# Groups that end a phase are read earlier, in banks and token halves, in a kernel of two transformer blocks

## The chip, the core and the metric

One core of one Trainium2 chip runs the whole program. Its engines are TensorE (PE), VectorE (DVE), ScalarE (ACT), GpSimd (POOL) and SyncE (SP, which only issues transfers). The metric is the device time of one execution in microseconds (us).

## What is computed

Two different transformer blocks follow each other on 256 tokens of width 2048, all in float32. Cut to what matters here:

```python
def first_block(x, p, ...):
    u = rms_norm(h, ln_mix_pre)
    hq, hf, hi, hg, aq, ak, av = split(u @ w_in)                    # 7 x 1024 columns
    mixed = concatenate([hgrn2(hq, hf, hi, hg), dilated_attention(aq, ak, av)]) @ w_out
    h = h + rms_norm(mixed, ln_mix_post)
    y = conv_gated_mlp(rms_norm(h, ln_ffn_pre), w_up, ..., w_down)  # hidden 5632
    h = h + rms_norm(y, ln_ffn_post)
    return h + (p @ w_pe) * sigmoid(h @ w_pg)

def second_block(x, p, ...):
    z = rms_norm(h, attn_norm_g) @ w_in                             # 5 x 1024 columns
    h = h + concatenate([diff_attention(...), gmlp_gate(...)]) @ w_out
    f = rms_norm(h, ffn_norm_g)
    h = h + (silu(f @ w1) * (f @ w3)) @ w2                          # hidden 5632
    h = h + (p @ pl_w_up) * sigmoid(h @ pl_w_gate)
    return rms_norm(h, final_norm_g)
```

The recurrence of `hgrn2` is computed over the whole sequence by levels: a level compares token spans half as long as the one before, its products are laid into one matrix of scores by `merge`.

## The kernel before

**Phases and chunks.** The weights pass once, in chunks of 1 MB (128 x 2048 values). `PHASES` lists them: `in1`, `out1`, `up`, `down1`, `pe1`, `down1b`, `pg1` for the first block; `in2`, `out2`, `glu`, `down2`, `pe2`, `down2b`, `pg2` for the second. A phase runs `iters` times over `body` chunks; `per` chunks, 4 or 11, make a group, whose sums stay in PSUM (the tensor `ps`, 8 banks of 512 values a partition) until it is complete.

**Each weight is split in two.** Factor and weight are each written as a high part, rounded to fp32r, plus a low part, the rest, and three of the products are summed. SP loads a chunk into one of four `raw` buffers; ACT rounds it into `w_hi` (`high`, L513); DVE subtracts into `w_lo` (`low`, L1370); PE multiplies. `w_hi` and `w_lo` have two buffers each, so the rounding of chunk c + 2 starts when chunk c is multiplied (semaphore `chunks_multiplied`), and must be through `low` before chunk c + 1 ends.

**Two layouts.** Column phases (`up`, `in2`, `glu`, the first four rounds of `in1`) put output columns on partitions: 32 matmuls a chunk, a group takes 4 banks (`by_columns`, L950 and L951). Row phases (the rest) put tokens on partitions: 24 matmuls a chunk, a group takes 2 banks, `2 * gr` for tokens 0 to 127 and the next for 128 to 255 (`by_rows`, L966 to L968, which does both halves for each row tile of weights).

**What reads a finished group.** `mixed_square` (ACT) and `mixed_gains` (DVE) in `out1`, `down1`, `down1b`; after the last of these, `token_sums`, `token_roots`, `inverse_roots`, `mixed_add`, then PE turns the new rows (`turn`, L926) and ACT and DVE split them (`turned_high`, `turned_low`) before the next phase can start. `add_rows` (DVE, L1965) in `out2`, `down2`, `down2b`. `sigmoid` (ACT, L805) and `gate` (DVE, L1839 and L1841) in `pg1`, `pg2`. Before PE writes a group, `group_free` waits until its banks are read.

**Order.** There is no scheduler: every engine runs its own hand-written list. `stream` on each engine walks the chunks j of a phase; on ACT it issues `high` for chunk j + 2 and then what the table `at` has for j; on DVE `low` for j + 2, then `at[j]`, then, where a group ends, the reading of it (`evac`); on PE `at[j]` stands before the matmuls of chunk j. `positions` does the same for `in1` with chunk numbers 0 to 55; `slot(l)` is 18 + 3(l - 1). `level(l)` on PE needs `factors(l)` and `merge(l - 1)`; `attention_scores(n)` needs banks 6 and 7 that `masked(n)` on DVE reads.

## Time and profile before

| | |
|---|---|
| median of 3 runs (lowest to highest) | 2556.55 us (2554.41 to 2558.72) |
| the profiled execution | 2555.99 us, span 2554.3 us |
| mean granted TensorE clock | 0.991 |
| PE busy | 2491.4 us, 98% of the span |
| DVE busy, ACT busy | 1489.6 us, 1096.5 us |
| share of the chain that ended last | PE 93%, DVE 3%, ACT 2% |

The span runs from the first to the last instruction of one profiled execution. "Busy" is the time in which an engine executes something; an engine with a lower share has idle time that costs nothing unless another engine waits for it. The granted clock is in shares of full speed.

### The profile page before, as it was taken

To read this page: it belongs to the slowest core of one execution; us is meant where nothing else is said; L and a number is where in the kernel's file an instruction comes from. 1 tells how busy PE (TensorE), PEld (TensorE's weight loads), DVE (VectorE), ACT (ScalarE), POOL (GpSimd) and SP (SyncE) were. 2 spreads that over 40 slices of the span, in tenths; PEclk is the share of its full clock that TensorE was granted. 3 is DMA by queue.
4 is the path that set the end of the run, shared out by engine and by line. 5 is a ranking of instruction groups with operands and counts; after the bars stand their busy time and mean duration, and the time that the engine had idled before them with its cause. 6 is when DMAs were issued, how large, how long until landed. Compare 5 with 4: busy or idle time off the path is not lost.

```text
span 2554.3 us, 31924 instructions
## 1 busy us (share of the span) xinstructions
PE 2491.4 (98%) x13381; PEld 2144.0 (84%) x13381; DVE 1489.6 (58%) x1069; ACT 1096.5 (43%) x916; POOL 188.7 (7%) x115
## 2 busy tenths in 40 slices
PE   7999999999999999999999999999999999999997
PEld 6998788788888888888788888778888888888886
DVE  5865635566677775444565757545555555545455
ACT  4533455544444444333454435344333333333344
POOL 2000000011212112000000000001121211100000
PEclk9999999999999999999999999999999999999999
DMA  6544455455555555655465554455556555555544
GB/s 230 190 142 140 142 172 181 159 187 184 194 185 193 186 192 186 213 183 196 148 222 162 185 170 144 148 165 183 196 183 194 184 194 186 197 181 198 184 179 148
DMA packets 230532, 460.04 MB, mean 180 GB/s; under 512 B 7526, under 2 KB 10540, under 8 KB 230060
## 3 DMA queue, kind: packets, MB, share of 16 engines
q1 hardware_dynamic: 230152, 458.71, 53.5%
q8 instruction: 69, 1.13, 0.2%
q14 instruction: 19, 0.16, 0.0%
q10 hardware_dynamic: 292, 0.04, 0.0%
HBM read 456.62 MB, written 2.10 MB: 180 GB/s over the span
## 4 chain that ended last, share of the span: by engine, by line
PE 93%; DVE 3%; ACT 2%; issue 1%; DMA 1%; POOL 0%; ACTq 0%; SPq 0%; POOLq 0%; DVEq 0%
PE ps L950 33%; PE ps L951 17%; PE ps L966 12%; PE ps L967 12%; PE ps L968 12%; ACT w_hi L513 1%; PE ps L957 1%; PE ps L959 1%; PE ps L958 1%; DVE w_lo L1370 1%; PE ps L1126 1%; PE ps L926 1%; PE ps L1133 0%; DMA raw<-in_w_down_dram 0%; DMA raw<-in_w_in_dram 0%
## 5 line engine op out<-in xcount | busy, mean ns | idle before, releaser
L1370 DVE TENSOR_TENSOR w_lo<-raw,w_hi 128x2048 fp32r<-128x2048 f32 x428 | 980.3, 2291 | 1010.0 <-ACT w_hi L513 1009.9
L513 ACT ACTIVATE w_hi<-raw 128x2048 fp32r<-128x2048 f32 x428 | 820.4, 1917 | 1372.9 <-PE ps L951 722.4
L950 PE MATMUL ps<-xa,w_hi 128*128 128x512 f32 x3072 | 1071.8, 395 | 12.4 <-DVE xa L1434 6.7
L951 PE MATMUL ps<-xa,w_lo 128*128 128x256 f32 x3072 | 853.7, 278 | 0.0
L950 PEld LDWEIGHTS ps<-xa,w_hi 128*128 128x128 f32 x3072 | 578.3, 188 | 147.6 <-DVE h L1965 5.9
L951 PEld LDWEIGHTS ps<-xa,w_lo 128*128 128x128 f32 x3072 | 579.5, 189 | 0.0
L966 PE MATMUL ps<-w_hi,g 128*128 128x512 f32 x1088 | 427.0, 393 | 2.1 <-DVE w_lo L1370 1.1
L968 PE MATMUL ps<-w_hi,g 128*128 128x512 f32 x1088 | 424.7, 390 | 0.0
L967 PE MATMUL ps<-w_lo,g 128*128 128x512 f32 x1088 | 424.7, 390 | 0.0
L966 PEld LDWEIGHTS ps<-w_hi,g 128*128 128x128 f32 x1088 | 205.2, 189 | 46.1 <-issue 3.0
L968 PEld LDWEIGHTS ps<-w_hi,g 128*128 128x128 f32 x1088 | 205.1, 189 | 43.0
L967 PEld LDWEIGHTS ps<-w_lo,g 128*128 128x128 f32 x1088 | 205.2, 189 | 42.0 <-issue 0.2
L950 PE MATMUL ps<-g,w_hi 128*128 128x512 f32 x640 | 227.8, 400 | 3.1 <-ACT ff L805 3.0
L478 POOL TENSOR_TENSOR ff<-ff 128x1024 f32<-128x1024 f32 x22 | 96.6, 4391 | 1526.6 <-DVE ff L1787 869.5
L951 PE MATMUL ps<-g,w_lo 128*128 128x256 f32 x640 | 179.6, 281 | 0.0
L950 PEld LDWEIGHTS ps<-g,w_hi 128*128 128x128 f32 x640 | 121.4, 190 | 32.5 <-ACT ff L805 3.4
L966 PE MATMUL ps<-w_hi,xa 128*128 128x512 f32 x320 | 126.4, 395 | 0.0
L967 PE MATMUL ps<-w_lo,xa 128*128 128x512 f32 x320 | 125.0, 391 | 0.0
L968 PE MATMUL ps<-w_hi,xa 128*128 128x512 f32 x320 | 125.0, 390 | 0.0
L951 PEld LDWEIGHTS ps<-g,w_lo 128*128 128x128 f32 x640 | 121.9, 190 | 0.3 <-issue 0.2
L1484 DVE TENSOR_REDUCE ff<-ps 128x1024 f32<-128x2048 f32 x44 | 100.5, 2284 | 0.0
L481 POOL TENSOR_TENSOR g<-ff,g 128x1024 f32 x22 | 74.4, 3382 | 107.0 <-ACT g L759 107.0
(275 smaller groups left out, 1599.5 us busy)
## 6 DMA issues: line engine op xcount, KB each, us to landing
raw<-in_ffn_w_dram SPq DMA_DIRECT2D x132, 1024.0 KB, 5.1
raw<-in_w_in_dram SPq DMA_DIRECT2D x96, 1024.0 KB, 5.1
raw<-in_w_up_dram SPq DMA_DIRECT2D x88, 1024.0 KB, 5.0
raw<-in_w_down_dram SPq DMA_DIRECT2D x44, 1024.0 KB, 5.0
raw<-in_w_out_dram SPq DMA_DIRECT2D x32, 1024.0 KB, 5.0
raw<-in_w_pg_dram SPq DMA_DIRECT2D x16, 1024.0 KB, 5.1
raw<-in_pl_w_gate_dram SPq DMA_DIRECT2D x16, 1024.0 KB, 5.9
raw<-in_w_pe_dram SPq DMA_DIRECT2D x2, 1024.0 KB, 4.8
```

The costliest lines, as they stand in the source:

```text
L478: pool.tensor_tensor(prod[:, :, :], ff_out[0][:, :, :], val[:, :, :], ALU.mult)\
L481: pool.tensor_tensor(g[:, bass.ds(i * 4, 4), S:2 * S], prod[:, :, :], g[:, bass.ds(i * 4, 4), 0:S].bitcast(F32), ALU.subtract).then_inc(se ...
L513: A(w_hi[j % SPLIT][:, :], raw[s][:, :], ACT.Copy).then_inc(sem("w_hi_ready"), 1)
L926: last = nc.tensor.transpose(bank(turn_bank(q), 2)[:, k * S + a * P:k * S + (a + 1) * P], h_rows[:, a, (4 * q + k) * P:(4 * q + k + 1) * P ...
L950: mm(ps[:, 4 * gr + n, :], hi[:, k, w], x, start=begin, stop=False)
L951: return mm(ps[:, 4 * gr + n, 0:S], lo[:, k, w], x[:, 0:S], start=False, stop=end)
L957: mm(o, hi[:, k, w], x[:, 0:S], start=begin and n % 2 == 0, stop=False, skip_group_check=True)
L966: mm(o, high, hi, start=begin, stop=False)
L967: mm(o, high, lo, start=False, stop=False)
L968: last = mm(o, low, hi, start=False, stop=end)
L1370: V.tensor_tensor(w_lo[j % SPLIT][:, :], raw[j % RAW][:, :], w_hi[j % SPLIT][:, :].bitcast(F32), ALU.subtract).then_inc(sem("w_lo_ready"), 1)
L1484: return V.tensor_reduce(dst, halves(gr).rearrange("p b (a t) -> p b t a", a=2), AX.X, ALU.add)
```

## The change

It moves instructions and waits; what is computed stays.

1. In the last chunk of every group of a row phase PE does all matmuls of the first token half, raises `half_multiplied`, then those of the second half. ACT's first square of a mixed group waits for that; both squares of a group now come before the gains of their bank, and after the last group of `out1` and `down1b` the second gain product stands behind the first `mixed_add`.
2. A column phase's first group waits at its start only for the older pair of the row phase's banks (`rows_done(ph, 3)`), and for the younger ones (`rows_done(ph, 4)`) before its third quarter, where it first writes them.
3. `stream(..., early=True)` on DVE (`out2`, `down2`, `down2b`): `add_rows` stands ahead of `low` where a group ends. In `pg1`, ACT's last sigmoid stands ahead of the last rounding.
4. In `in1` the attention scores move from positions 33, 36, 39 to 34, 37, 40, behind the level there; `masked` and the last `merge` move with them.
5. The last group of `pg2` is read in halves, and two of the four stores of the output are issued by ACT instead of SP.

```diff
-            def mixed_square(name, n, gr, chunks):
+            def mixed_square(name, n, gr, chunks, half):
 
                 m = 4 * (name == "down1") + n
                 o = square_out[name]
                 if n:
                     act.wait_ge(sem("mixed_squared"), 2 * m)
+                act.wait_ge(sem("half_multiplied"), half)
+                A(o[:, 0:512], bank(2 * gr), ACT.Square, accum_out=sum_at(name, 0, n)).then_inc(sem("mixed_squared"), 1)
                 act.wait_ge(sem("chunks_multiplied"), chunks)
-                A(o[:, 0:512], bank(2 * gr), ACT.Square, accum_out=sum_at(name, 0, n)).then_inc(sem("mixed_squared"), 1)
-                act.wait_ge(sem("mixed_gained"), m + 1)
...
-                41: lambda: exponentials(2, p0),
+                42: lambda: exponentials(2, p0),
...
-            stream("pg1", unroll=True, started=True, at={
+            stream("pg1", unroll=True, started=True, late=True, at={
                 0: steps({1: lambda: row_squares("in2", 1)}),
                 1: steps({1: lambda: turned_high("in2", 1)}),
                 3: lambda i: sigmoid("pg1", 2 * i),
                 4: lambda i: row_squares("in2", 2 * i),
                 5: lambda i: turned_high("in2", 2 * i),
-                7: lambda i: sigmoid("pg1", 2 * i + 1)})
+                7: steps({0: lambda: sigmoid("pg1", 1)})})
+            sigmoid("pg1", 3)
+            high("pg1", 1, 9)
...
-                7: lambda i: sigmoid("pg2", 2 * i + 1)})
+                7: steps({0: lambda: sigmoid("pg2", 1)})})
+            act.wait_ge(sem("h_ready"), H_READY["out"] + 2)
+            for a in range(2):
+                act.wait_ge(*((sem("chunks_multiplied"), done("pg2", 1, 7)) if a else (sem("half_multiplied"), HALVES["pg2"] + 4)))
+                A(sigmoids["pg2"][1][:, 512 * a:512 * (a + 1)], bank(2 + a), ACT.Sigmoid).then_inc(sem("last_sigmoid"), 1)
             root_table()
-            row_squares("out", 3)
+            act.wait_ge(sem("rows_squared"), ROWS_SQUARED["out"] + 3)
+            for a in range(2):
+                act.wait_ge(sem("last_added"), a + 1)
+                A(square_out["out"][:, 512 * a:512 * (a + 1)], row_quad(h_rows, 3)[:, a, :], ACT.Square, accum_out=sum_at("out", a, 3))\
+                    .then_inc(sem("last_squared"), 1)
...
+                act.wait_ge(sem("out_rows"), half + 1)
+                act.dma_start(out[0, P:S, half * 1024:(half + 1) * 1024], o).then_inc(sem("out_stored"), 16)
...
-                    pe.wait_ge(*{"up": (sem("factor_ready"), FACTOR["up"] + 1), "in2": (sem("sigmoid_done"), 4),
-                                 "glu": (sem("h_ready"), H_READY["glu"] + 4)}[ph])
+                    rows_done(ph, 3)
...
+                            if begun and ph in COLUMN_PHASES and (j, n) == (0, 2):
+                                rows_done(ph, 4)
                             if begun and ph in COLUMN_PHASES and (j, n) == (4, 3):
                                 pe.wait_ge(sem("scale_ready"), SPREAD[ph])
+                            if rows and q < per - 1:
+                                for a in range(2):
+                                    last = by_rows(2 * gr, x[:, x0 + n, :], hi[:, n, :], lo[:, n, :], q == 0 and n == 0, False, a)
+                                continue
+                            if rows and n % 2 == 0:
+                                for k in range(4):
+                                    last = by_rows(2 * gr, x[:, x0 + k, :], hi[:, k, :], lo[:, k, :], False, k == 3, n // 2)
+                                if n == 0:
+                                    last.then_inc(sem("half_multiplied"), 1)
...
-                33: lambda: attention_scores(0),
-                slot(5) + 4: lambda: level(5),
-                36: lambda: attention_scores(1),
-                slot(6) + 4: lambda: level(6),
-                39: lambda: attention_scores(2),
-                slot(7) + 4: lambda: level(7),
+                slot(5) + 4: lambda: (level(5), attention_scores(0)),
+                slot(6) + 4: lambda: (level(6), attention_scores(1)),
+                slot(7) + 4: lambda: (level(7), attention_scores(2)),
...
+            def mixed_gain(name, n, gr, a):
 
                 m = 4 * (name == "down1") + n
                 c = slice(512 * n, 512 * (n + 1))
+                dve.wait_ge(sem("mixed_squared"), 2 * m + a + 1)
+                last = V.tensor_tensor(y_rows[name][:, a, c], bank(2 * gr + a), gain_row[name][:, c], ALU.mult)
+                if a:
+                    last.then_inc(sem("mixed_read"), 1)
+
+            def mixed_gains(name, n, gr):
+
                 dve.wait_ge(sem("gain_row_landed"), 16 * GAIN_ROW_NO[name])
-                V.tensor_tensor(y_rows[name][:, 1, c], bank(2 * gr + 1), gain_row[name][:, c], ALU.mult).then_inc(sem("mixed_gained"), 1)
-                dve.wait_ge(sem("mixed_squared"), 2 * m + 1)
-                V.tensor_tensor(y_rows[name][:, 0, c], bank(2 * gr), gain_row[name][:, c], ALU.mult).then_inc(sem("mixed_read"), 1)
-                if n == 3:
-                    dve.wait_ge(sem("mixed_squared"), 2 * m + 2)
-                    token_sums(name)
+                mixed_gain(name, n, gr, 0)
+                if n < 3:
+                    return mixed_gain(name, n, gr, 1)
+                dve.wait_ge(sem("mixed_squared"), 8 * (name == "down1") + 8)
+                token_sums(name)
...
+                        if early and j % per == per - 1:
+                            dve.wait_ge(sem("chunks_multiplied"), chunk_no(ph, i, j) + 1)
+                            evac(i, j // per)
...
-                34: lambda: (factors(6), masked(1, p1[:, 0:4, :], S)),
-                35: lambda: merge(5),
+                34: lambda: factors(6),
+                35: lambda: (masked(1, p1[:, 0:4, :], S), merge(5)),
                 slot(7): lambda: relative(7),
-                37: lambda: (factors(7), masked(2, p1[:, 4:8, :], S)),
-                38: lambda: merge(6),
+                37: lambda: factors(7),
+                38: lambda: (masked(2, p1[:, 4:8, :], S), merge(6)),
                 39: lambda: maxima(2, p1, 8),
-                40: lambda: (masked(3, p0, P), maxima(3, p0, 0)),
-                41: lambda: merge(7),
+                41: lambda: (masked(3, p0, P), maxima(3, p0, 0), merge(7)),
...
+            mixed_gain("out1", 3, 1, 1)
...
+            stream("out2", lambda i, gr: add_rows("out2", 2 * i + gr, gr), unroll=True, started=True, early=True,
...
+            stream("pg2", lambda i, gr: gate("pg2", 2 * i + gr) if (i, gr) != (1, 1) else None,
...
-            final_gain(3).then_inc(sem("final_gained"), 1)
-            row_sums("out")
+            for a in range(2):
+                dve.wait_ge(sem("last_sigmoid"), a + 1)
+                g3 = sigmoids["pg2"][1][:, 512 * a:512 * (a + 1)]
+                then(V.tensor_tensor(g3, g3, pe_rows["pe2"][3][:, 512 * a:512 * (a + 1)], ALU.mult))
+                hq = row_quad(h_rows, 3)[:, a, :]
+                V.tensor_tensor(hq, hq, g3, ALU.add).then_inc(sem("last_added"), 1)
+            for a in range(2):
+                dve.wait_ge(sem("last_added"), a + 1)
+                last = V.tensor_tensor(row_quad(final_rows, 3)[:, a, :], row_quad(h_rows, 3)[:, a, :],
+                                       gain_row["out"][:, 1536:2048], ALU.mult)
+            last.then_inc(sem("final_gained"), 1)
+            dve.wait_ge(sem("rows_squared"), ROWS_SQUARED["out"] + 3)
+            dve.wait_ge(sem("last_squared"), 2)
+            token_sums("out")
```

**in1.** PE at positions 33 and 34 before; L1133 are the scores, L1126 a level, L966 to L968 a chunk.

```order
L968 MATMUL ps<-w_hi,xa 128x512
L1133 MATMUL ps<-g_work 128x256 [waits level_merged,banks_read]
L1133 MATMUL ps<-g_work 128x256 x3
L966 MATMUL ps<-w_hi,xa 128x512 [waits w_lo_ready,factor_ready]
...
L1126 MATMUL ps<-g_work 128x64 [waits level_merged,level_factors]
L1126 MATMUL ps<-g_work 128x64 x15
```

The same place of the changed kernel, and its position 37; L1153 is a level there, L1160 the scores, L976 to L978 a chunk.

```order
L978 MATMUL ps<-w_hi,xa 128x512
L1153 MATMUL ps<-g_work 128x64 [waits level_merged,level_factors]
L1153 MATMUL ps<-g_work 128x64 x15
L1160 MATMUL ps<-g_work 128x256 [waits level_merged,banks_read]
L1160 MATMUL ps<-g_work 128x256 x3
L976 MATMUL ps<-w_hi,xa 128x512 [waits w_lo_ready,factor_ready]
...
L1153 MATMUL ps<-g_work 128x64 [waits level_merged,level_factors]
L1153 MATMUL ps<-g_work 128x64 x15
L1160 MATMUL ps<-g_work 128x256 [waits att_masked]
L1160 MATMUL ps<-g_work 128x256 x3
```

The scores stand behind the level. On DVE, positions 34 and 35 before: L1631 and L1632 are `factors`, L1665 `masked`, L1370 `low`, L1650 `merge`.

```order
L1370 TENSOR_TENSOR w_lo<-raw,w_hi 128x2048 [waits w_hi_ready]
L1631 TENSOR_TENSOR g_work<-g_work,ff 128x512x2 [waits level_decay]
L1632 TENSOR_TENSOR g_work<-g_work 128x512x2
L1665 SCALAR_TENSOR_TENSOR ff<-ps,g_work 128x1024 [waits att_scores]
L1370 TENSOR_TENSOR w_lo<-raw,w_hi 128x2048 [waits w_hi_ready]
L1650 COPY_PREDICATED g_work<-g_work,ps 128x256x4 [waits level_merged,level_done]
```

And of the changed kernel, where these are L1664 and L1665, L1698, L1394 and L1683:

```order
L1394 TENSOR_TENSOR w_lo<-raw,w_hi 128x2048 [waits w_hi_ready]
L1664 TENSOR_TENSOR g_work<-g_work,ff 128x512x2 [waits level_decay]
L1665 TENSOR_TENSOR g_work<-g_work 128x512x2
L1394 TENSOR_TENSOR w_lo<-raw,w_hi 128x2048 [waits w_hi_ready]
L1698 SCALAR_TENSOR_TENSOR ff<-ps,g_work 128x1024 [waits att_scores]
L1683 COPY_PREDICATED g_work<-g_work,ps 128x256x4 [waits level_merged,level_done]
```

`masked` is now behind the next `low`, directly ahead of `merge`.

**out2 to glu.** DVE at the end of `out2` before; L1965 is `add_rows`, L1434 the split of a factor for `glu`.

```order
L1434 SCALAR_TENSOR_TENSOR xa<-ps,cols,xa 128x256 [waits factor_high]
L1434 SCALAR_TENSOR_TENSOR xa<-ps,cols,xa 128x256 x3
L1370 TENSOR_TENSOR w_lo<-raw,w_hi 128x2048 [waits w_hi_ready] x2
L1965 TENSOR_TENSOR h<-h,ps 128x2x512 [waits chunks_multiplied]
L1370 TENSOR_TENSOR w_lo<-raw,w_hi 128x2048 [waits w_hi_ready]
L1434 SCALAR_TENSOR_TENSOR xa<-ps,cols,xa 128x256 [waits factor_high]
L1434 SCALAR_TENSOR_TENSOR xa<-ps,cols,xa 128x256 x3
```

Of the changed kernel, with `add_rows` as L1999 and the split as L1464:

```order
L1464 SCALAR_TENSOR_TENSOR xa<-ps,cols,xa 128x256 [waits factor_high]
L1464 SCALAR_TENSOR_TENSOR xa<-ps,cols,xa 128x256 x3
L1394 TENSOR_TENSOR w_lo<-raw,w_hi 128x2048 [waits w_hi_ready]
L1999 TENSOR_TENSOR h<-h,ps 128x2x512 [waits chunks_multiplied]
L1394 TENSOR_TENSOR w_lo<-raw,w_hi 128x2048 [waits w_hi_ready] x2
L1464 SCALAR_TENSOR_TENSOR xa<-ps,cols,xa 128x256 [waits factor_high]
L1464 SCALAR_TENSOR_TENSOR xa<-ps,cols,xa 128x256 x3
```

`add_rows` stands ahead of one of the two `low` that it was behind.

**pg1 to in2.** ACT at the end of `pg1` before; L805 is the sigmoid, L513 `high`.

```order
L513 ACTIVATE w_hi<-raw 128x2048 [waits chunks_multiplied,raw_landed0]
L513 ACTIVATE w_hi<-raw 128x2048 [waits chunks_multiplied,raw_landed1]
L805 ACTIVATE ff<-ps 128x1024 [waits h_ready,chunks_multiplied]
L513 ACTIVATE w_hi<-raw 128x2048 [waits chunks_multiplied,raw_landed2]
L554 ACTIVATE g<-ps,cols 128x256 [waits turned]
```

Of the changed kernel, with the sigmoid as L804 and `high` as L512:

```order
L512 ACTIVATE w_hi<-raw 128x2048 [waits chunks_multiplied,raw_landed0]
L804 ACTIVATE ff<-ps 128x1024 [waits h_ready,chunks_multiplied]
L512 ACTIVATE w_hi<-raw 128x2048 [waits chunks_multiplied,raw_landed1]
L512 ACTIVATE w_hi<-raw 128x2048 [waits chunks_multiplied,raw_landed2]
L553 ACTIVATE g<-ps,cols 128x256 [waits turned]
```

The last sigmoid is ahead of the last `high` of `pg1`.

## Rows read from the trace of the kernel before

**Rows 1.** The page: busy time and instructions of PE.

```profile
PE 2491.4 (98%) x13381; PEld 2144.0 (84%) x13381; DVE 1489.6 (58%) x1069; ACT 1096.5 (43%) x916; POOL 188.7 (7%) x115
```

**Rows 2.** PE's waits: line, for whom, us in total, times, longest.

```profile
PE ps L926 <- DVE h L1416: 7.5, 2, 3.8
...
PE ps L950 <- DVE h L1965: 5.5, 1, 5.5
PE ps L950 <- ACT ff L805: 3.0, 1, 3.0
PE ps L1133 <- DVE ff L1665: 2.4, 1, 2.4
PE ps L1139 <- DVE ff L1665: 2.4, 1, 2.4
PE ps L1133 <- DVE g_work L1560: 2.3, 1, 2.3
...
PE ps L966 <- DVE ff L1808: 1.2, 1, 1.2
```

**Rows 3.** Windows: us; PE, PEld, DVE, ACT, POOL busy; PE clock; DMA share, GB/s.

```profile
233.80:238.50 4.70, 4.67 (x14) 3.77 (x15) 3.35 (x2) 0.00 (x0) 0.00 (x0) 0.64 0.47 144
1345.20:1351.20 6.00, 5.94 (x19) 5.07 (x20) 4.00 (x5) 0.01 (x1) 0.96 (x3) 0.50 0.61 200
1706.40:1709.60 3.20, 3.18 (x10) 2.69 (x11) 0.00 (x0) 0.00 (x0) 0.00 (x0) 0.50 0.96 310
2548.00:2553.30 5.30, 0.00 (x0) 0.00 (x0) 0.00 (x0) 0.74 (x1) 0.00 (x0) 0.50 0.98 391
```

**Rows 4.** Timeline, out2 to glu: start, us, engine, line, operation, [idle before].

```profile
1701.00 1.91 ACT L513 ACTIVATE w_hi<-raw 128x2048 fp32r<-128x2048 f32 x1 [3.52 <-PE ps L968]
...
1702.95 2.29 DVE L1370 TENSOR_TENSOR w_lo<-raw,w_hi 128x2048 fp32r<-128x2048 f32 x1 [3.14 <-ACT w_hi L513]
1705.15 1.21 DVE L1965 TENSOR_TENSOR h<-h,ps 128x1024 f32<-128x1024 f32 x1
```

**Rows 5.** Timeline, pg1 to in2, and a later chunk of in2.

```profile
1344.20 1.00 ACT L805 ACTIVATE ff<-ps 128x1024 f32<-128x1024 f32 x1
...
1344.33 2.29 DVE L1370 TENSOR_TENSOR w_lo<-raw,w_hi 128x2048 fp32r<-128x2048 f32 x1 [3.14 <-ACT w_hi L513]
...
1347.79 1.23 DVE L1841 TENSOR_TENSOR h<-h,ff 128x1024 f32<-128x1024 f32 x1
...
1377.53 1.92 ACT L513 ACTIVATE w_hi<-raw 128x2048 fp32r<-128x2048 f32 x1 [3.63 <-PE ps L951]
```

**Rows 6.** Timeline of DVE in in1: mask of the scores, and merges.

```profile
235.90 1.25 DVE L1650 COPY_PREDICATED g_work<-g_work,ps 128x1024 f32<-128x1024 uint32 x1
...
258.48 1.22 DVE L1665 SCALAR_TENSOR_TENSOR ff<-ps,g_work 128x1024 f32<-128x1024 f32 x1
...
261.81 1.26 DVE L1650 COPY_PREDICATED g_work<-g_work,ps 128x1024 f32<-128x1024 uint32 x1
...
286.15 2.46 DVE L1650 COPY_PREDICATED g_work<-g_work,ps 128x1024 f32<-128x1024 uint32 x1
```

**Rows 7.** Timeline of ACT and DVE, out1 to up.

```profile
486.66 0.60 ACT L533 ACTIVATE g_work<-ps 128x512 f32<-128x512 f32 x1 [2.01 <-PE ps L968]
...
487.32 0.60 ACT L535 ACTIVATE g_work<-ps 128x512 f32<-128x512 f32 x1
...
488.77 4.06 DVE L1416 SCALAR_TENSOR_TENSOR h<-g_work,tok,h 128x512 f32<-128x512 f32 x6
493.19 1.66 DVE L1434 SCALAR_TENSOR_TENSOR xa<-ps,cols,xa 128x256 fp32r<-128x256 f32 x4 [0.35 <-ACT xa L554]
```

**Rows 8.** Timeline of the end; issues of the stores (ns min/median/max).

```profile
2540.76 1.02 ACT L805 ACTIVATE g_work<-ps 128x1024 f32<-128x1024 f32 x1 [8.90 <-PE ps L968]
...
2545.83 0.16 DVE L1378 TENSOR_REDUCE tok<-tok 128x2 f32<-128x8 f32 x1 [0.20 <-ACT g_work L543]
...
L380 SPq DMA_DIRECT2D out_dram<-g_work x4: 357/608/1191, 2547.3 to 2549.0; - x4
```

More of the change, by code:

```diff
@@ L29 @@
 NORMS = {"out1": 6, "down1": 20, "up": 34, "in2": 48, "glu": 62, "out": 76}
+HALVES = {"out1": 6, "down1": 10, "down1b": 12, "pg1": 14, "out2": 18, "down2": 22, "down2b": 24, "pg2": 26}
 NORM_NO = {"out1": 1, "up": 2, "down1": 3, "in2": 4, "glu": 5, "out": 6}
@@ L376, in _ @@
             for half in range(2):
[L377 to L381 removed]
+                sp.wait_ge(sem("out_rows_too"), half + 1)
+                c = slice(half * 1024, (half + 1) * 1024)
+                sp.dma_start(out[0, 0:P, c], final_rows[:, 0, c]).then_inc(sem("out_stored"), 16)
             sp.wait_ge(sem("out_stored"), 64)
@@ L959, in by_narrow_columns, with by_rows @@
                 return mm(o, lo[:, k, w], x[:, 0:S], start=False, stop=end, skip_group_check=True)
[L961 to L969 removed]
+            def by_rows(b, x, hi, lo, begin, end, a):
+                high, low = x[:, a * P:(a + 1) * P], x[:, S + a * P:S + (a + 1) * P]
+                o = bank(b + a)
+                mm(o, high, hi, start=begin, stop=False)
+                mm(o, high, lo, start=False, stop=False)
+                return mm(o, low, hi, start=False, stop=end)
             def mixed_done(n):
@@ L1447, in first, with stream @@
                 return lambda i: f() if isinstance(i, int) and i == 0 else None
-            def stream(ph, evac=None, peel=0, at=None, unroll=False, tail=0, started=False, before=None):
+            def stream(ph, evac=None, peel=0, at=None, unroll=False, tail=0, started=False, before=None, early=False):
                 pl = plan[ph]
@@ L1476, in body @@
                             at[j](i)
-                        if evac and j % per == per - 1:
+                        if evac and not early and j % per == per - 1:
                             dve.wait_ge(sem("chunks_multiplied"), chunk_no(ph, i, j) + 1)
```

47 lines of the change are left out of this document (19 added, 28 removed).

## The prediction

> **What bounds the kernel now.** I read the page first: PE is busy 2491.4 us of 2554.3 [rows 1], so what a change of order can win is in the 63 us in which PE has nothing, and in stretches at the lower clock. The table of PE's waits names them [rows 2]: 5.5 us at the first chunk of `glu` for `add_rows` (L1965), 3.0 at the first of `in2` for the last sigmoid (L805), 2.4, 2.4 and 2.3 at the attention scores in `in1`, 7.5 in two waits for `mixed_add` (L1416, borders `out1`/`up` and `down1b`/`pg1`), 1.2 in `pe2`. Then the windows behind three of these waits, for what a wait costs once it is over [rows 3]: after the wait in `in2` PE runs 6.0 us at granted clock 0.50, the lower of its two levels (1.2 of 2.4 GHz); after that in `glu` 3.2 us at 0.50; after the first score wait 4.7 us at 0.64. Half of 6.0 is lost, 3.0 us; half of 3.2, 1.6; and 0.36 of 4.7, 1.7. So a wait that goes takes such a stretch with it.
>
> **The grid.** At `out2`'s last chunk ACT starts the next rounding at 1701.00, 1.91 long after 3.52 idle: a row chunk is 5.43 us, and this start marks its end within 0.1 [rows 4]. DVE starts `low` 1.95 later and its next instruction 4.15 after the mark. A column chunk is 1.92 + 3.63 = 5.55 [rows 5].
>
> **out2 to glu** [rows 4]. Before, `low` stands ahead of `add_rows`, which ends at 1706.4. With `early` it stands first: from 1701.0 to 1702.2, while DVE would wait for ACT until 1702.95 anyway, so `low` isn't moved. PE now asks at its start only for the older pair of banks, and for the other after half a chunk, at 1703.7, when it has been free for 1.5 us. The next chunk's `w_lo` comes at 1705.2 and is needed at 1706.4. Wait 5.5 and slow stretch 1.6 go: **7.1 us**. If the order were back, 5.4 less half a chunk (2.8) would still wait.
>
> **pg1 to in2** [rows 5]. The last chunk of `pg1` ended 1.95 before `low` started, at 1342.4. With `late`, the sigmoid of 1.0 stands first on ACT, and ends at 1343.4; PE asks for it only half a chunk on, at 1345.1. Queued behind it are the last rounding of `pg1`, 0.9 later than before, then `low` (to 1347.5), the load that SP starts when `low` frees its raw buffer (wanted three chunks later), and the gate, two instructions of 1.23, which now ends at 1349.9 instead of 1349.0. PE reaches its second chunk at 1342.2 + 5.55 = 1347.75: 0.2 us in hand. `turn("in2", 3)`, a chunk and a half after the start, is at 1350.5 and needs the gate of 1349.9: 0.6 in hand. Wait 3.0 and slow stretch 3.0 go: **6.0 us**. What is late next is this turn; a slip there would cost its own size.
>
> **in1** [rows 4, 6]. All three waits for scores go (2.3 + 2.4 + 2.4 = 7.1), and so does the slow stretch of 1.7. But the merge of a level is now behind `masked` on DVE, and `level` is the next thing PE wants. One chunk's mark is 0. `low` runs from 1.95 to 4.15, `masked` takes 1.2 (L1665) to 5.3, and `merge(5)` with its 1.26 ends at 6.55; PE is at `level(6)` at 5.35, so it waits 1.2. `merge(6)` is 2.46 long, so `level(7)` waits 2.4. `merge(4)`, which before lay under a wait, ends at 237.15, and PE without that wait is there at 236.9 (231.5 + 5.43): 0.2. At position 41 `masked`, `maxima` and `merge(7)` (1.2, as much for `maxima`, which reads as many elements, and 2.4 by the row of `merge(6)`) now follow each other: the next `low` starts at 9.0 and ends at 11.3, and is needed at 10.8: 0.5. New waits are 4.3 us. Net 7.1 + 1.7 - 4.3 = **4.5 us**; 2.8 if the wait of 2.4 drops the clock as the first one did. The scores themselves, 8 to 16 matmuls, are the same in number. Two similar waits of 2.4 dropped nothing, so I take 4.5.
>
> A rule for this, in sentences of their own. The Trainium skill, TensorE: Matmul & The Clock Gate, section "Part 1: The HAM clock gate", says that the number of slow matmuls after a start is run-variable, one kernel showing 6, 11 or 14. The trace agrees: the wait of 3.0 us cost 3.0 in clock, that of 5.5 only 1.6. By the rule the 6.3 us of clock in my sum are one draw, and another execution could lose two more or less.
>
> **out1 to up, down1b to pg1** [rows 7]. The two squares of the last group start 0.66 us apart (486.66, 487.32). With the first bank finished half a chunk earlier, only the second follows the last matmul, so the sums come 0.66 sooner. But one of the two gain products moves behind the first `mixed_add`: 0.68 more among the six adds of 0.68 (4.06 / 6), ahead of `turned_low`. At `up`, `turned_low` stood 0.35 idle for ACT after the adds (L1434) and can start 0.3 earlier: **0.3 us**. At `pg1` ACT's part is one instruction for four, so that DVE, with its longer queue, is the later: **0**. Bounds for each are 0 and 0.66. The waits of up to 3.8 and their slow clock stay.
>
> **down2 to pe2** [rows 2]. `add_rows` leaves the queue ahead of the first copy out of the banks (L1808), which so comes 1.1 us earlier; of the wait of 1.2 some 0.05 stays: **1.1 us**. In `pe1` the products are still behind `low`, and the wait of 1.2 stays. `down2b` has no wait to lose.
>
> **The end** [rows 8]. The last sigmoid is split, but DVE's stream still waits for the whole last chunk before it turns to either half. From 2540.76 it then has four half-width products and sums of 0.70 each (0.68 for the adds of that width in [rows 7], and a wait on the one before), to 2543.5, and two gain products of some 0.65, to 2544.8; `token_sums` stood at 2545.83. ACT's table load and its two squares fit beside (the last square follows the last sum and ends at 2544.3). So **1.0 us**. The stores: two of four now go from ACT. The output leaves at DMA share 0.98 from 2548.0 to 2553.3 [rows 3], so more issuers add nothing, and the first issue is SP's in both; the second ACT product now starts after an issue (0.36 to 1.2 us), yet its data is wanted only 4 us into the stores. Nothing lost or won; bounds -0.5 and +1. The Trainium skill, DMA: Bandwidth & Descriptors, section "Issuing engines are not separate DMA queues", says the same: only the sequencer's time for the issue is saved.
>
> **Last chunks by token halves.** 30 chunks of 24 matmuls stay as many, but a bank now takes 12 in a row instead of 3. Column chunks keep a bank for 8 and need 5.55 for the columns that a row chunk does in 5.43 [rows 4, 5]; laid wholly on this, it is 0.12 x 30 = 3.6 us at most. The other reading, that the 32 instead of 24 instructions make it, is as near: I take 0 and keep 3.6 for the range.
>
> **Sum.** 7.1 + 6.0 + 4.5 + 0.3 + 0 + 1.1 + 1.0 = 20.0 us. The profiled execution has 2555.99 (span 2554.3), 0.56 under the median of the runs shown, 2556.55. Less 20.0: 2536.0, and on the median's footing **2536.5 us**.
>
> **Rivals.**
> - The clock: the new wait of 2.4 in `in1` brings its own slow stretch (1.7), or a border that now runs through still drops. 2538 to 2541. One wait of three such did; chance 0.2.
> - Moved waits: the small margins of 0.2 and 0.6 at `in2` don't hold, or the last chunks cost up to 3.6. For it speaks that DVE is there nearly continuously in use; against it that a slip costs only itself. 2538 to 2540; chance 0.1.
> - The borders are given back: PE starts `glu` and `in2` early but stands later for the scale, which hangs on the same row sums. Then 7.1 + 6.0 return: 2549.6. Against it: the last turn stands at PE's own position in the second chunk and starts that chain, before and after. Chance 0.05.
> - No effect (within 0.2%, 5.1 us, about what a measurement of this kernel can tell): the above and the clock together; 0.03.
> - Slower: long runs in one bank slow the matmuls in the last chunks. To eat 20 us it must cost 0.67 us in each of 30, 28 ns on a step of 227; to be slower by 5.1, 35 ns, and then 2562. The column chunks, with runs of 8, show at most 5 ns. Chance 0.02.
> - Better than forecast: stores on two queues, and clock at the borders of `up` and `pg1`, some 1 to 3 us: 2534. Chance 0.1.
>
> The forecast as worked out, 2535 to 2538, has 0.5. The range 2532.5 to 2541.5 takes in the clock, the moved waits and the better case. Faster 0.95, same 0.03, slower 0.02.
>
> **What would show it.** In the table of waits, the rows of L1965 and L805 are gone, and PE's first `glu` and `in2` windows are at clock 1.0. In `in1` the score rows are gone, and `level` waits for the merge (COPY_PREDICATED) twice, 1.2 and 2.4 us. `mixed_add` still holds 6 to 7 us. The span from the last matmul to the end is 1 us shorter. I am wrong if PE waits at a later chunk of `in2` or `glu`, if row chunks that end a group last over 5.5 us, or if `level` waits show a granted clock under 1.

## The result and the profile after

| | before | after |
|---|---|---|
| median (lowest to highest), 5 runs each | 2558.56 us (2554.41 to 2559.83) | 2544.37 us (2543.28 to 2546.19) |
| the profiled execution | 2555.99 us, span 2554.3 | 2543.82 us, span 2542.1 |
| mean granted TensorE clock | 0.991 | 0.990 |

The ratio is 0.9949, interval [0.9934, 0.9963]: faster, by less than forecast. On the two profiled executions it is 12.2 us instead of 20.0. The page of the kernel after, then its table of PE's waits (line, what it waited for, us in total, times, longest):

```profile
PE 2492.3 (98%) x13381; PEld 2146.2 (84%) x13381; DVE 1490.2 (59%) x1072; ACT 1096.6 (43%) x917; POOL 193.1 (8%) x115
```

```profile
PE ps L961 <- DVE xa L1464: 7.3, 3, 3.5
...
PE ps L937 <- DVE h L1446: 6.9, 3, 3.0
PE ps L1153 <- DVE g_work L1683: 4.2, 3, 2.5
PE ps L1345 <- ACT xa_work L855: 2.1, 1, 2.1
PE ps L1355 <- ACT ff L871: 2.0, 1, 2.0
PE ps L976 <- DVE w_lo L1394: 2.0, 3, 0.9
...
PE ps L976 <- DVE xa_work L1841: 1.2, 1, 1.2
```

Against [rows 2]: `add_rows` and the sigmoid are gone, so is the `ff` of `pe2`, and so are the three scores. New is `level` (L1153) waiting for `merge` (L1683), 4.2 us in three waits where 3.8 were forecast; the waits of row chunks for `w_lo` grew from 1.1 to 2.0, by 0.9 with 0.5 forecast. PE is busy 0.9 us longer than in [rows 1], though its matmuls are as many: some of them ran slower.

**Where the 12.2 us are.** Every chunk has one rounding on ACT, so the starts of the 428 roundings are one scale for both traces. The difference of these starts (after less before), taken between stretches:

| stretch | forecast | measured |
|---|---|---|
| `in1` | -4.5 | +2.7 |
| border of `up` | -0.3 | +0.7 |
| `up` to `down1b`, border of `pg1` | 0 | +0.2 |
| border of `in2` | -6.0 | -5.9 |
| within `in2` and `out2` | 0 | -0.6 |
| border of `glu` | -7.1 | -7.1 |
| `pe2` | -1.1 | -1.1 |
| behind the last rounding | -1.0 | -1.2 |
| ahead of `in1`'s levels | 0 | +0.2 |

The sum is -12.1. Of the 7.8 us that are missing to the forecast of 20.0, 7.2 are in `in1`.

**The two borders.** Timelines of ACT after, and windows, one at the start of `in2` and two from the start of `glu` on (us; busy PE, PEld, DVE, ACT, POOL; granted clock; DMA share; GB/s):

```profile
1346.12 1.03 ACT L804 ACTIVATE ff<-ps 128x1024 f32<-128x1024 f32 x1 [3.46 <-PE ps L978]
1347.04 1.91 ACT L512 ACTIVATE w_hi<-raw 128x2048 fp32r<-128x2048 f32 x1
1351.82 1.92 ACT L512 ACTIVATE w_hi<-raw 128x2048 fp32r<-128x2048 f32 x1 [2.87 <-PE ps L962]
...
1698.24 1.92 ACT L512 ACTIVATE w_hi<-raw 128x2048 fp32r<-128x2048 f32 x1 [3.52 <-PE ps L978]
1703.88 1.92 ACT L512 ACTIVATE w_hi<-raw 128x2048 fp32r<-128x2048 f32 x1 [3.72 <-PE ps L962]
```

```profile
1344.00:1350.00 6.00, 6.00 (x33) 5.12 (x32) 2.00 (x2) 2.83 (x2) 0.00 (x0) 1.00 0.54 175
```

```profile
1698.20:1703.00 4.80, 4.80 (x29) 4.19 (x28) 3.49 (x2) 1.92 (x1) 0.00 (x0) 1.00 0.66 217
1703.00:1709.00 6.00, 6.00 (x39) 5.31 (x38) 2.29 (x1) 3.40 (x6) 0.00 (x0) 1.00 0.57 178
```

At `glu` one rounding follows the other after 5.64 us; in [rows 4] PE had still to wait and to run slowly. PE is busy without a gap over both borders, at clock 1.00 instead of 0.50 [rows 3].

**in1.** Before, the waits of 2.4 us ahead of the second and the third scores were followed by no slow stretch. Two windows of before, each over such a wait, the scores and the chunk:

```profile
257.40:267.20 9.80, 7.45 (x34) 6.25 (x35) 5.68 (x5) 3.06 (x3) 0.00 (x0) 1.00 0.64 213
281.70:291.60 9.90, 7.54 (x43) 6.54 (x43) 6.92 (x5) 1.91 (x1) 0.00 (x0) 1.00 0.64 211
```

After: the timeline of PE at the three levels, the wait for DVE's `merge` in brackets, and windows over the second and third:

```profile
237.48 2.75 PE L1153 MATMUL ps<-g_work 128*128 128x64 f32 x23 [0.35 <-DVE g_work L1683]
...
260.74 3.63 PE L1153 MATMUL ps<-g_work 128*128 128x64 f32 x25 [1.35 <-DVE g_work L1683]
...
265.67 3.72 PE L1160 MATMUL ps<-g_work 128*128 128x256 f32 x8
...
288.49 5.54 PE L1153 MATMUL ps<-g_work 128*128 128x64 f32 x32 [2.53 <-DVE g_work L1683]
```

```profile
257.00:261.00 4.00, 2.65 (x14) 1.94 (x12) 3.59 (x3) 1.63 (x2) 0.00 (x0) 1.00 0.40 115
260.70:266.00 5.30, 5.26 (x33) 5.29 (x34) 4.50 (x3) 0.69 (x1) 0.00 (x0) 0.70 0.57 187
266.00:270.00 4.00, 4.00 (x11) 3.14 (x11) 0.06 (x1) 0.00 (x0) 0.00 (x0) 0.54 0.56 215
270.00:275.00 5.00, 5.00 (x24) 4.11 (x23) 0.00 (x0) 0.00 (x0) 0.00 (x0) 1.00 0.02 3
284.00:288.40 4.40, 1.95 (x9) 1.30 (x7) 4.40 (x4) 2.35 (x2) 0.00 (x0) 1.00 0.53 162
288.40:294.00 5.60, 5.51 (x33) 5.54 (x34) 4.25 (x2) 0.71 (x2) 0.00 (x0) 0.66 0.56 183
294.00:298.00 4.00, 4.00 (x21) 3.87 (x21) 0.00 (x0) 0.00 (x0) 0.00 (x0) 0.63 0.24 91
```

The waits are the forecast ones (0.35, 1.35, 2.53 against 0.2, 1.2, 2.4). But behind the second and the third PE runs 9 us at 0.54 to 0.70. The 8 score matmuls take 3.72 us there and 1.95 behind the first. Taken from the start of one rounding on ACT (259.48) to the next (275.17), this chunk with its level and scores lasts 15.69 us, 14.34 without the wait; in experiment 2, where the same work runs at full clock, it is 11.21 less a wait of 0.22, so 10.99. The stretch costs 3.35 us. At the third place it is 16.84 less 2.53 against 12.48 less 1.41: 3.2 us. These 6.6 us, the 0.4 by which the three waits came out longer than forecast, and 0.3 more than forecast in the wait for `w_lo` are the 7.2 that are missing in `in1`.

### The profile page after: what moved, and what is told of

Same layout as the page of the kernel before. It is cut to its first block, busy times and chain, and to the rows that moved or that the text cites. A ratio compares the mean times of both kernels' runs of the same rounds, so it can differ in the third digit from the quotient of the medians.

```text
span 2542.1 us, 31931 instructions
## 1 busy us (share of the span) xinstructions
PE 2492.3 (98%) x13381; PEld 2146.2 (84%) x13381; DVE 1490.2 (59%) x1072; ACT 1096.6 (43%) x917; POOL 193.1 (8%) x115
## 4 chain that ended last, share of the span: by engine, by line
PE 94%; DVE 3%; ACT 2%; issue 1%; DMA 1%; POOL 0%; SPq 0%; ACTq 0%; POOLq 0%; DVEq 0%
PE ps L961 33%; PE ps L962 17%; PE ps L976 12%; PE ps L978 12%; PE ps L977 12%; ACT w_hi L512 1%; PE ps L1153 1%; PE ps L968 1%; PE ps L970 1%; PE ps L969 1%; DVE w_lo L1394 1%; PE ps L937 1%; PE ps L1160 0%; DVE g_work L1683 0%; DMA raw<-in_w_down_dram 0%
## 5 line engine op out<-in xcount | busy, mean ns | idle before, releaser
L1394 DVE TENSOR_TENSOR w_lo<-raw,w_hi 128x2048 fp32r<-128x2048 f32 x428 | 980.4, 2291 | 989.1 <-ACT w_hi L512 988.8
L512 ACT ACTIVATE w_hi<-raw 128x2048 fp32r<-128x2048 f32 x428 | 820.6, 1917 | 1372.1 <-PE ps L962 709.4
L976 PE MATMUL ps<-w_hi,g 128*128 128x512 f32 x1088 | 427.0, 392 | 2.4 <-DVE w_lo L1394 1.5
L978 PE MATMUL ps<-w_hi,g 128*128 128x512 f32 x1088 | 424.5, 390 | 0.0
L976 PEld LDWEIGHTS ps<-w_hi,g 128*128 128x128 f32 x1088 | 205.1, 189 | 46.0 <-issue 3.3
L978 PEld LDWEIGHTS ps<-w_hi,g 128*128 128x128 f32 x1088 | 205.1, 189 | 43.2
L976 PE MATMUL ps<-w_hi,xa 128*128 128x512 f32 x320 | 126.0, 394 | 0.5 <-DVE w_lo L1394 0.5
L978 PE MATMUL ps<-w_hi,xa 128*128 128x512 f32 x320 | 124.6, 389 | 0.0
```

The source lines that it names most:

```text
L512: A(w_hi[j % SPLIT][:, :], raw[s][:, :], ACT.Copy).then_inc(sem("w_hi_ready"), 1)
L976: mm(o, high, hi, start=begin, stop=False)
L978: return mm(o, low, hi, start=False, stop=end)
L1394: V.tensor_tensor(w_lo[j % SPLIT][:, :], raw[j % RAW][:, :], w_hi[j % SPLIT][:, :].bitcast(F32), ALU.subtract).then_inc(sem("w_lo_ready"), 1)
```

## The experiments

Each kernel was timed in turn with the kernel before, on the same chip, in one of four sessions, in which the kernel before had medians of 2557.25 to 2559.02 us. There are five executions where nothing else is said. Medians are given with the ratio to before; what is said of a part comes from the starts of the roundings in the profile.

**1. The order of in1, undone and alone.** The first kernel is the changed one with the positions of before in `in1`, on DVE too; the second is the kernel before with only the new ones.

```diff
...
-                slot(5) + 4: lambda: (level(5), attention_scores(0)),
-                slot(6) + 4: lambda: (level(6), attention_scores(1)),
-                slot(7) + 4: lambda: (level(7), attention_scores(2)),
+                33: lambda: attention_scores(0),
+                slot(5) + 4: lambda: level(5),
+                36: lambda: attention_scores(1),
...
```

> The changed kernel with the schedule of in1 as before: scores at positions 33, 36, 39, masked and merge as they stood. Theory A (the order in in1 loses: four waits of 4.2 us in sum and two stretches at a granted clock of 0.54 to 0.70 that cost 3.3 to 3.4 us each, against 7.1 of waits and 1.7 of clock before): the start of the first rounding of up comes 2.7 us earlier than in the changed kernel, and the time is about 2541.6 us, 17 under before. Rival B (in1 is later by 3 us for another reason, above all the last chunks by token halves, which in1's row groups have too): the time stays at 2544 and the 3 us are still there at up.

> The kernel before with the changed schedule of in1 alone (scores behind the levels at 34, 37, 40, masked and merge(7) moved, exponentials at 42). Theory A: 2.7 us slower than before, with waits for merge of about 0.3, 1.3 and 2.4 us ahead of the levels and a granted clock under 0.8 in the 8 to 10 us behind two of them. Rival B: no slower than before, or faster by the 4.5 us that were forecast for this term.

Undone: 2543.11 us, 0.9944 [0.9931, 0.9958]. `in1` takes exactly what it took before (-0.01), 2.7 less than in the changed kernel. The whole gained only 1.3 us in the median. The profiled execution, the longest of the five (2544.72), shows why it isn't 2.7 there: it is 2.0 later than the changed kernel's already ahead of the levels, and loses 2.3 more within `in2` and `out2`, where nothing is changed. Alone (eleven executions): 2560.74 us, 1.0014 [1.0005, 1.0023], and `in1` is longer by 2.73 us with the waits 0.35, 1.37 and 2.54. Theory A holds on the part; rival B is out. The part that was to give 4.5 us makes the kernel slower.

**2. Scores first; merge first.** With the same pair of level and scores at one position, only the order on PE or on DVE is turned round.

```diff
-                slot(5) + 4: lambda: (level(5), attention_scores(0)),
+                slot(5) + 4: lambda: (attention_scores(0), level(5)),
...
```

```diff
-                35: lambda: (masked(1, p1[:, 0:4, :], S), merge(5)),
+                35: lambda: (merge(5), masked(1, p1[:, 0:4, :], S)),
...
-                38: lambda: (masked(2, p1[:, 4:8, :], S), merge(6)),
+                38: lambda: (merge(6), masked(2, p1[:, 4:8, :], S)),
```

> The changed kernel with the scores ahead of the level at positions 34, 37 and 40, nothing else. The scores need only masked, which DVE ends about when PE gets there; they last 1.95 us, and the merge that the level wants (5 and 6) ends 1.2 and 2.4 us after masked. Theory A, in which the wait directly ahead of level and scores drops the clock: waits of 0, 0 and about 0.4 us, granted clock 1.00 in these stretches, 4.2 - 0.4 + 6.7 = 10.5 us less than the changed kernel, about 2534. Rival C (level and scores back to back leave PE so thinly used that the clock falls with or without a wait): the waits go, 3.8 us, but the two stretches of 3.4 stay, about 2540.5.

> The changed kernel with merge(5) and merge(6) ahead of masked on DVE, nothing else. The level then waits 0.1 at position 37 instead of 1.35 and 1.25 at 40 instead of 2.45. Theory A: the stretch at the lower clock at 37 goes (3.4) and that at 40 goes or stays: 2.5 of waits and 3.4 to 6.7 of clock, 2535 to 2538.5. Rival C (the clock falls with the adjacency of level and scores, whatever the wait): only the 2.5 us of waits go, about 2542.

Scores first: 2535.09 us, 0.9914 [0.9901, 0.9928]. `in1` is 10.2 us shorter than in the changed kernel, with 10.5 expected. Its rows at the third place, and windows:

```profile
281.57 2.05 PE L1166 MATMUL ps<-g_work 128*128 128x128 f32 x16
284.04 3.76 PE L1153 MATMUL ps<-g_work 128*128 128x64 f32 x32 [0.42 <-DVE g_work L1683]
```

```profile
261.00:266.00 5.00, 5.00 (x40) 4.78 (x39) 4.42 (x3) 0.48 (x1) 0.00 (x0) 1.00 0.54 172
...
284.00:288.00 4.00, 3.96 (x34) 3.95 (x35) 4.00 (x2) 0.64 (x2) 0.00 (x0) 1.00 0.41 112
```

The same 32 matmuls that took 5.54 us take 3.76. The scores want only `masked`, and while they run (2.05 us in the row above) the merge goes on. Merge first: 2536.11 us, 0.9924 [0.991, 0.9937], waits of 0.35, 0.22 and 1.41, clock 1.00 at all three, `in1` 8.8 us shorter. Level and scores stand back to back in both kernels without a drop, which is the end of rival C.

**3. One merge first at a time.** The edit of the first kernel; the second has the same at 35, with `merge(5)`.

```diff
...
-                38: lambda: (masked(2, p1[:, 4:8, :], S), merge(6)),
+                38: lambda: (merge(6), masked(2, p1[:, 4:8, :], S)),
```

> The changed kernel with merge(6) alone ahead of masked: the level at 37 still waits 1.35 us, that at 40 waits 1.4 instead of 2.5. Theory A, as the runs so far leave it (a wait of 1.35 at 37 dropped the clock each time, one of 1.4 at 40 did not in the only profile that has it): the stretch at 37 stays with its 3.3 us, that at 40 goes, 1.1 + 3.4 = 4.5 us faster than the changed kernel, 2540. Rival E (the two stretches hang together, the second comes because the first was there): both stay, 1.1 us faster. Rival D (chance): anything, and the executions scatter by 3 us.

> The changed kernel with merge(5) alone ahead of masked: the level at 37 waits 0.2 us instead of 1.35, that at 40 still 2.5. Theory A: the stretch at 37 goes, that at 40 stays with its 3.3 us, 1.1 + 3.4 = 4.5 us faster than the changed kernel, 2540. Rival E (the second stretch comes because the first was there): both go, 7.9 us faster, 2536.5. Rival D (chance): executions scatter by 3 us.

With `merge(6)` first: 2540.77 us, 0.9939 [0.9925, 0.9952], as expected, but not by the mechanism: in the profiled execution (2538.73) neither stretch is there, though the wait of 1.37 us at 37 is. The five executions lie between 2536.07 and 2544.72 us, which fits a stretch that comes in some of them and not in others. Two windows over the second place:

```profile
261.70:264.30 2.60, 2.58 (x23) 2.60 (x24) 1.84 (x1) 0.66 (x1) 0.00 (x0) 1.00 0.79 306
...
265.30:267.30 2.00, 2.00 (x11) 1.79 (x11) 1.73 (x2) 0.00 (x0) 0.00 (x0) 1.00 0.62 155
```

With `merge(5)` first: 2540.32 us, 0.9938 [0.9925, 0.9952]; clock 1.00 at 37, and the stretch behind the wait of 2.54 stays. So the second doesn't need the first (rival E is out). Its level at 40:

```profile
285.95 2.37 PE L1153 MATMUL ps<-g_work 128*128 128x64 f32 x10 [2.54 <-DVE g_work L1683]
287.69 5.32 PE L1153 MATMUL ps<-g_work 128*128 128x64 f32 x24
```

```profile
287.70:293.00 5.30, 5.30 (x26) 5.30 (x26) 2.41 (x2) 0.00 (x0) 0.00 (x0) 0.50 0.61 198
```

**4. What must stand behind the wait.** The first kernel takes the scores away from behind the level and keeps the waits; the second keeps the waits and lets the scores have them, with the level behind (both edits of experiment 2 at once). The end of the first edit:

```diff
...
-                slot(7) + 4: lambda: (level(7), attention_scores(2)),
+                slot(7) + 4: lambda: level(7),
+                41: lambda: attention_scores(2),
```

> The changed kernel with the scores one chunk later than the levels (positions 35, 38, 41), DVE's order as in the changed kernel. The waits of 0.35, 1.35 and 2.5 us ahead of the levels stay, but behind each level stands a full chunk, and the scores come a chunk later without a wait. Theory F (a wait directly ahead of a level drops the clock by itself): the stretches at 37 and 40 stay, 6 to 7 us, time as the changed kernel, 2544 to 2546. Theory G (it takes the wait and behind it level and scores together): the stretches go or shrink to those of a level alone, about 2538.

> The changed kernel with the scores ahead of the levels on PE, and merge(5) and merge(6) ahead of masked on DVE: now the scores wait, by DVE's rows 1.2 and 2.4 us, and level and chunk follow. The pair is the same, only the order behind the wait is turned round. Theory F (it is the level that must not stand directly behind a wait): granted clock 1.00 behind them, only the waits of 3.6 us remain, about 3.2 us slower than with masked first, 2538.5. Theory G (the pair behind a wait of this length drops the clock in either order): stretches of 3.3 come back at one or both places, 2542 to 2545.

The first: 2544.41 us, 0.9949 [0.9935, 0.9962]. In its profile (2541.86 us, the lowest of the five executions) nothing drops behind the wait of 1.35 us, and behind that of 2.53, with a level alone and a full chunk after it, the stretch is there:

```profile
285.00:289.00 4.00, 3.19 (x25) 3.21 (x25) 4.00 (x3) 1.45 (x3) 0.00 (x0) 0.89 0.43 155
289.00:293.00 4.00, 4.00 (x15) 3.52 (x15) 0.97 (x1) 0.00 (x0) 0.00 (x0) 0.50 0.77 257
```

The second: 2537.65 us, 0.992 [0.9907, 0.9934]; nothing behind the wait of 1.24, but behind that of 2.37 ahead of the scores the clock falls all the same:

```profile
284.92 2.62 PE L1166 MATMUL ps<-g_work 128*128 128x128 f32 x16 [2.37 <-DVE ff L1698]
```

```profile
284.90:289.00 4.10, 4.08 (x25) 4.09 (x25) 4.10 (x2) 0.81 (x2) 0.00 (x0) 0.66 0.40 116
289.00:295.00 6.00, 6.00 (x27) 5.83 (x27) 0.25 (x1) 0.00 (x0) 0.00 (x0) 0.50 0.41 155
```

Neither theory is right as it was put. F fails in the second kernel, where the level isn't the one that waits, and G in the first, where the pair is apart. But the second kernel's median, 2537.65, is the number of F (2538.5, no stretch) and not of G (2542 to 2545), and its profile is of the longest of the five executions (2539.81): whether the other four had the stretch isn't known. All profiles of the study together, one execution of each kernel:

| wait of PE in `in1`, and what follows | stretches at the lower clock |
|---|---|
| 0.2 to 0.4 us, then a level | 0 of 15 |
| 1.24 to 1.41 us, then level and/or scores | 6 of 11 |
| 2.4 to 2.5 us, then level, level and scores, or scores and level | 9 of 9, 3.2 to 4.9 us each |
| 2.3 to 2.4 us, then scores and a full chunk (order of before) | 2 of 6, up to 1.7 us each |

A level lies behind every one of the third row. The six of the second row are one schedule, that of the change at position 37, which had the wait of 1.35 to 1.37 with level and scores behind it in seven profiles; in the seventh, that of experiment 3, nothing dropped. The other four of the row, with 1.41 at 40 or another order, dropped nothing. So the row says that such a wait can drop the clock, not how often a schedule will.

**5. The borders, one step at a time.**

```diff
-            stream("out2", lambda i, gr: add_rows("out2", 2 * i + gr, gr), unroll=True, started=True, early=True,
+            stream("out2", lambda i, gr: add_rows("out2", 2 * i + gr, gr), unroll=True, started=True,
...
```

```diff
-                    rows_done(ph, 3)
+                    rows_done(ph, 4)
```

> The changed kernel with add_rows behind low again in out2, down2 and down2b; the wait per bank pair stays. Theory (the two steps at glu add up): add_rows then ends 5.4 us after PE's mark, PE needs the younger banks 2.8 us after it, so a wait of 2.6 to 2.8 us comes back inside the first glu chunk, and in pe2 the wait of 1.2. Together 3.9 us slower than the changed kernel, up to 5.5 if a stretch at the lower clock follows. Rival (the wait per bank pair alone does it, low's order is not needed): no slower than the changed kernel at glu.

> The changed kernel in which up, in2 and glu wait at their start for all banks of the row phase before; the reading stays ahead of low and of the last rounding. By DVE's and ACT's rows the readers end 1.2 us (glu) and 1.0 us (in2) after PE's mark: two waits of about 1.2 and 1.2 us come back, 2.4 us slower than the changed kernel. Each may bring a stretch at the lower clock of 1.6 to 3.0 us, then up to 7 us slower. Rival (PE has other work queued there that hides it): no change.

Without `early` (eleven executions): 2552.38 us, 0.9968 [0.9959, 0.9978]. The first row below is the wait inside `glu`'s first chunk, 2.7 us where 2.6 to 2.8 were expected, the second the old one in `pe2`:

```profile
PE ps L961 <- DVE h L1999: 2.7, 1, 2.7
...
PE ps L976 <- DVE ff L1841: 1.2, 1, 1.2
```

The border of `glu` loses 4.5 us (the wait, and 1.8 of clock behind it) and `pe2` 1.1, together 5.6, where at most 5.5 was expected. The medians lie 8.0 apart, and 6.4 if the changed kernel is taken from the same session (experiment 6); the two profiles lie 8.6 apart, and the 3.0 beyond the 5.6 are at places that the edit doesn't touch. Two of the executions took 2543.56 and 2544.41, the others 2550.19 to 2553.05; which place made them shorter isn't known, since neither was profiled. Waiting for all banks: 2547.93 us, 0.9961 [0.9947, 0.9974], 2.0 to 3.6 slower than the changed kernel in its two measurements. Three rows:

```profile
PE ps L1355 <- ACT ff L871: 2.9, 1, 2.9
...
PE ps L961 <- DVE h L1999: 1.3, 1, 1.3
...
PE ps L961 <- ACT ff L804: 1.1, 1, 1.1
```

The two waits are those expected. Each border loses 0.3 more than its wait, and not by the clock: no stretch at the lower clock follows either of them. A third comes unannounced: a wait at the end of `in2` (L1355) grows from 2.0 to 2.9. So both steps are needed, and they are worth what the chain of the forecast gave them.

**6. Halves, and the change once more.**

```diff
...
-                                for k in range(4):
-                                    last = by_rows(2 * gr, x[:, x0 + k, :], hi[:, k, :], lo[:, k, :], False, k == 3, n // 2)
...
+                                for a in range(2):
+                                    last = by_rows(2 * gr, x[:, x0 + n, :], hi[:, n, :], lo[:, n, :], False, n == 3, a)
...
```

> The changed kernel with the last chunks of row groups in the order of before, both token halves for each row tile; half_multiplied is raised by the last matmul of the first half, three matmuls ahead of the end. What reads in halves then starts half a chunk later. Forecast by the prediction: the runs of 12 in one bank cost nothing, so the chunks last as long, and the time grows only by what the halves gave: up to 0.7 us at the border of up, nothing at pg1, and some 0 to 0.6 us at the end, 0.3 to 1.5 us slower together. Rival (the runs of 12 do cost, up to 0.12 us in each of 30 chunks): up to 3.6 us faster in the chunks, which gives a faster kernel.

> The changed kernel, unaltered, a second time, for how far the stretches at the lower clock repeat. Theory A: the wait of 1.35 us ahead of the level at position 37 and that of 2.5 at position 40 are each followed by 7 to 9 us at a granted clock of 0.5 to 0.7 again, start of up 3 us later than before. Rival D (the stretches fall here or there by chance): one or both are at clock 1.00 this time, and the time is 3.4 or 6.7 us shorter in that profile.

Without halves: 2544.05 us, 0.9948 [0.9934, 0.9961]. The last chunk of `out2` lasts 5.44 us in both orders and before. Runs of 12 in one bank cost nothing; the halves gave nothing either, where 0.3 to 1.5 us was expected of them: the border of `up` is within 0.2 us, the end within 0.1. The change again: 2545.94 us, 0.9951 [0.9938, 0.9965], both stretches in `in1` there again, `in1` +2.8.

**7. A version that beats both.** The scores first as in 2; `merge(7)` at position 44; in `pg2` DVE doesn't wait for the whole last chunk before the first half of the gate. In the second kernel the gain product behind the first `mixed_add` also moves behind the first `turned_low`, at both borders. Each was executed four times.

```diff
...
-                41: lambda: (masked(3, p0, P), maxima(3, p0, 0), merge(7)),
+                41: lambda: (masked(3, p0, P), maxima(3, p0, 0)),
...
+                44: lambda: merge(7),
...
-                        if evac and not early and j % per == per - 1:
+                        if evac and not early and j % per == per - 1 and not (last and i == 1 and j == 7):
...
-            mixed_gain("out1", 3, 1, 1)
             mixed_add("out1", 1)
             mixed_add("out1", 2)
             turned_low("up", 0)
+            mixed_gain("out1", 3, 1, 1)
```

> The changed kernel with the scores ahead of the levels, merge(7) at position 44 instead of 41, and no wait of DVE for the whole last chunk of pg2 ahead of the first half of the last gate. Against the kernel with the scores first alone (2535.1): the next low after position 41 starts 2.4 us earlier and the wait for w_lo of about 1 us goes; at the end two products and sums of 0.70 move under the last half chunk, 1.4 us. Forecast 2532.7. Rival: DVE's extra 2.4 at position 44 makes a later low late (then 2533.7), or the end hangs on ACT's table load and squares (then 2534).

> The same, and the second gain product of the last group of out1 and of down1b moved from behind the first mixed_add to behind the first turned_low. It takes 0.68 of DVE's time off the way to the first turned_low, whose start has 0.35 to 0.48 us of idle for ACT ahead of it: forecast 0.2 to 0.7 us earlier at up and as much at pg1, 2532 together. Rival (ACT's part, which waits for PE's turns at the lower clock, decides when PE can start): no gain, 2532.7.

2533.67 us, 0.9908 [0.9892, 0.9923], and 2532.71 us, 0.9906 [0.9891, 0.9922]; both end clear of the changed kernel's 0.9949 [0.9934, 0.9963], but not of the scores first alone, 0.9914 [0.9901, 0.9928]. The moved merge gave 0.1 instead of 1.0 (the waits for `w_lo` fell only from 2.1 to 1.6), the end 0.4 instead of 1.4. There the rival held; ACT's timeline of the first:

```profile
2521.14 1.28 ACT L516 ACT_TABLE_LOAD   x1
...
2522.54 0.61 ACT L909 ACTIVATE g_work<-h 128x512 f32<-128x512 f32 x1
...
2523.15 0.61 ACT L909 ACTIVATE g_work<-h 128x512 f32<-128x512 f32 x1
```

The table load stands behind the last sigmoid in ACT's list, and both squares behind the load, though the first sum is ready at 2519.9. The later gain product shows 0.6 us at `up` and 0.5 at `pg1`; the two medians lie 0.96 apart, less than this measurement can tell by itself.

## Why the prediction was wrong

The step that failed is in the term of `in1`, where the clock behind the moved waits was put at nothing: "Two similar waits of 2.4 dropped nothing, so I take 4.5."

- **in1 (forecast -4.5, measured +2.7).** The waits were right to 0.4 us each. Wrong was to carry the clock over from waits ahead of scores and a full chunk to waits ahead of a level. The change moves every wait to where the thin work stands: 32 matmuls of 64 columns, and the scores behind them. There a wait of 2.4 to 2.5 brought a stretch in every profile, and it cost 3.2 us and more, not the 1.7 that was the only price in view. A wait of 1.24 to 1.41 brought one in six of eleven profiled cases. The rival "the clock" named the mechanism and had both its number and its price too low: one of 1.7 where one of 3.35 and one of 3.2 came. By the forecast's own reading one wait of three had dropped the clock, and that was no odd draw: a second profile of the old order (experiment 1) has one of three again, at another wait. So even for the old order nothing was too little. The last of the forecast's own signs of being wrong, `level` waits with a granted clock under 1, is what came.
- **The pair's order.** The change puts the level, whose `merge` comes last on DVE, ahead of the scores, which need only `masked`. Turned round, waits and stretches are gone, and the median is 9.3 us lower.
- **in2, glu, pe2, the end (forecast 6.0, 7.1, 1.1, 1.0; measured 5.9, 7.1, 1.1, 1.2).** Right as sums, and at `glu` and `pe2` step by step: undone singly, the steps give back the waits that the timeline said. At `in2` only the wait per bank pair was undone by itself; the early sigmoid and the edits of the end were not, so for them the number agrees and the step isn't shown. The slow stretches of 3.0 and 1.6 went with their waits. The margins of 0.2 and 0.6 at `in2` held.
- **up (forecast -0.3, measured +0.7).** The wait for `mixed_add` shrank from 3.8 to 3.0, but between 492 and 500 us PE had a granted clock of 0.50, where it had 0.63 before. Over the 11 profiles that have this border just as changed, the difference is between -1.6 and +1.1, mean +0.1: the forecast can't be told from nothing there.
- **Runs of 12 in a bank** at 0: right, 5.44 us a chunk.
- **The clock as a draw.** The stretch within `in2` and `out2`, untouched in all kernels but the one that waits for all banks, lies between -0.6 and +1.7 us from before. The rule that the forecast cited from the Trainium skill, TensorE: Matmul & The Clock Gate, section "Part 1: The HAM clock gate" (the number of slow matmuls varies from run to run), is stated there for the start of a kernel; the trace agrees with it in the middle of one, by these numbers. The same page's section "HAM oscillation — how this bites in real kernels" tells of short batches of matmuls, each behind a wait of 3 to 5 us for a transfer, that run at the lower clock, and advises an order of the work in which PE doesn't stand waiting between them. The trace agrees that the batch behind the wait is slow, with 5.54 against 3.76 us for the same level, but here waits of 2.53 and 1.35 us were enough.

## What to carry to other kernels

- A wait has two prices: its length, and the stretch at the lower clock behind it. The second differed here with what PE did next: 9 of 9 with a level of small matmuls close behind the wait of 2.4 us, 2 of 6 with scores and a full chunk. Look at what stands behind the new place of a wait. A full chunk behind the level didn't help (experiment 4); hiding the wait did (experiment 2).
- When two steps share a position, put first the one whose input is ready first: here that alone gave 9 us.
- One profile is a single draw of each stretch. A sum that rests on "it dropped nothing here" needs the range of the other draw, for every wait of the kind.
